# Second attention of a two-block kernel: pairs of heads, the sink as a column of the scores, outputs scaled in place of probabilities, and the exchange between two scans behind the third pair

## The chip, the cores and the metric

One core of one Trainium2 chip runs the whole program. Its engines are TensorE (PE, with its weight loads shown apart as PEld), VectorE (DVE), ScalarE (ACT), GpSimd (POOL) and SyncE (SP). The metric is the device time of one execution in microseconds (us).

## The reference

Two transformer-like blocks run one behind the other on x of 256 positions by 2048 channels, all in float32. The change touches the second block alone, which projects the normed x to queries (16 heads of 64), two key/value heads, a 512-wide input u of a state-space model and two sets of 2048 gates. Its attention looks back 127 positions, adds a linear bias by distance, and has one learned sink per head, which takes part in the softmax but has no value:

```python
scores = einsum(q, kx) * (HEAD_DIM ** -0.5) + alibi           # masked outside the window
m = jnp.maximum(jnp.max(scores, axis=-1, keepdims=True), sink)
p = jnp.exp(scores - m)
p = p / (jnp.sum(p, axis=-1, keepdims=True) + jnp.exp(sink - m))
out = einsum(p, vx)
```

The state-space model is a linear recurrence over the 256 positions with 32 groups of 64 complex states, then an output projection, GELU, a gated linear unit and a branch projection. Attention output and model output are projected, gated, summed, projected again and added to x. A feed-forward network and a norm follow.

## The kernel before

**Panels and pieces.** All large products are cut into panels of 512 output columns, and a panel into pieces of two 128-row slices of the weights. Each float32 weight is split in two parts that a fast product can take: ScalarE copies the rounded part (`weights_hi`, L1100), VectorE subtracts it from the weight to get the rest (`weights_lo`, L1617, both inputs in SBUF), and TensorE makes three products of each slice for each half of the positions (L558 to L560). A whole piece is 12 matmuls, 128x512 each. The splits run three pieces ahead of TensorE (`AHEAD`), in rings of four.

**Side work.** Small work (norms, transposes, attention, scans' inputs) is written as generators, one for each engine, and each engine advances its generator by one step behind each piece (`side.step()`). The order on every engine is thus fixed in the program, and a step that waits holds all that stands behind it on its engine: on TensorE the next piece, on ScalarE and VectorE the next split. `side.finish()` runs what is left.

**The part around the change.** Behind the panels for u, q, k and v come eight panels of gates (`gate_attn`, `gate_ssm`), 64 pieces. Side work `attention2` begins at the first of them. I number these steps from 1. Steps 1 to 4 transpose q, step 6 transposes k, and from step 7 `attention` treats the heads one by one: a step with the scores (L744, L745), a step with the output product of the head before (L765, L766), and a step that transposes the probabilities (L580). Within the step of the scores VectorE adds the bias (L1880), takes the row maxima (L1884), scales them and compares them with the sink (L1889, L1891). ScalarE takes the sink's exponential (L1317) and the exponentials with their row sums (L1320). VectorE adds the sink's part to the sum (L1898), inverts it (L1899) and multiplies the probabilities (L1901), before TensorE may transpose them. After the output product ScalarE and VectorE copy the result as two parts (L1334, L1909).

**The scans.** GpSimd makes the recurrence, in two halves, since the states fill their tile (`ssm_states`): `scan(0)`, then `scan(1)`. Each has 15 steps over all blocks, 15 small steps along the blocks, and 16 long products over 900 elements (L446, L448), all with both inputs in SBUF. Between them stands the exchange, `ssm_halves`, six steps: two output products of the first half (L944, L945, which wait for `scanned`), then four input products of the second (L927, L928), whose copies by ScalarE (L1457) release `scan(1)`. `attention` runs it behind head 8 (`if interlude and h == MIDWAY`), in steps 35 to 40. Attention's last step is 61. After the gates come two panels of four pieces (`branch_attn[0]`, `[1]`), and behind the first piece of `branch_attn[2]` `ssm_end` waits for the second scan:

```python
    def ssm_output(self, half):
        pe, ev, m = self.pe, self.ev, self.m
        pe.wait_ge(ev["scanned"], half + 1)
```

## Time and profile before

| | |
|---|---|
| median of 3 runs | 2967.99 us (2964.32 to 2967.99) |
| the profiled execution's own time | 2966.49 us |
| its span | 2965.2 us |
| PE busy | 2906.5 us (98%) |
| DVE busy | 1673.1 us (56%) |
| ACT busy | 1323.0 us (45%) |
| POOL busy | 285.3 us (10%) |
| mean granted clock of TensorE | 0.993 of full speed |
| DMA | 536.74 MB, 181 GB/s on the mean |

The span is that of one profiled execution, from its first to its last instruction. Busy time is the union of an engine's instructions, so 98% for TensorE leaves 59 us of idle time, wherever it lies. In the chain of the work that ended last TensorE holds 89%, POOL 4%, DVE 3% and ACT 2%.

### The profile page before, as it was taken

To read this page: it belongs to the slowest core of one execution; us is meant where nothing else is said; L and a number is where in the kernel's file an instruction comes from. 1 tells how busy PE (TensorE), PEld (TensorE's weight loads), DVE (VectorE), ACT (ScalarE), POOL (GpSimd) and SP (SyncE) were. 2 spreads that over 40 slices of the span, in tenths; PEclk is the share of its full clock that TensorE was granted. 3 is DMA by queue.
4 is the path that set the end of the run, shared out by engine and by line. 5 is a ranking of instruction groups with operands and counts; after the bars stand their busy time and mean duration, and the time that the engine had idled before them with its cause. 6 is when DMAs were issued, how large, how long until landed. Compare 5 with 4: busy or idle time off the path is not lost.

```text
span 2965.2 us, 32189 instructions
## 1 busy us (share of the span) xinstructions
PE 2906.5 (98%) x13246; PEld 2377.5 (80%) x13246; DVE 1673.1 (56%) x1935; ACT 1323.0 (45%) x1639; POOL 285.3 (10%) x369
## 2 busy tenths in 40 slices
PE   9999999999999999999999999996999999999998
PEld 7888887888888888888888887674788888888886
DVE  4464655555555455455555567673755666656444
ACT  5444445444444444444444454343554444444443
POOL 0000000000000000000000069296100000000000
PEclk9999999999999999999999999998999999999999
DMA  7545453555555555555666554442655555555563
GB/s 244 188 168 198 157 187 130 178 191 199 185 190 180 197 185 189 194 185 188 189 198 196 197 170 148 154 162 86 205 181 189 178 191 185 184 189 187 191 199 128
DMA packets 278464, 536.74 MB, mean 181 GB/s; under 512 B 17250, under 2 KB 19742, under 8 KB 278318
## 3 DMA queue, kind: packets, MB, share of 16 engines
q1 hardware_dynamic: 266688, 528.52, 53.3%
q10 hardware_dynamic: 11629, 6.17, 0.8%
q8 instruction: 105, 1.72, 0.2%
q14 instruction: 42, 0.34, 0.0%
HBM read 532.55 MB, written 2.10 MB: 180 GB/s over the span
## 4 chain that ended last, share of the span: by engine, by line
PE 89%; POOL 4%; DVE 3%; ACT 2%; issue 1%; DMA 0%; ACTq 0%; SPq 0%; DVEq 0%
PE panels L558 29%; PE panels L560 28%; PE panels L559 28%; PE side L580 2%; DVE weights_lo L1617 2%; POOL scan_step L423 1%; POOL ssm_states L431 1%; POOL scan_step L426 1%; POOL ssm_states L430 1%; POOL ssm_states L448 1%; ACT weights_hi L1100 1%; POOL ssm_scratch L446 1%; DMA weights<-in_w_in 0%; ACT squares L1189 0%; PE side L765 0%
## 5 line engine op out<-in xcount | busy, mean ns | idle before, releaser
L1617 DVE TENSOR_TENSOR weights_lo<-weights,weights_hi 128x1024 fp32r<-128x1024 f32 (+1 forms) x1032 | 1262.2, 1229 | 1038.4 <-ACT weights_hi L1100 1035.0
L1100 ACT ACTIVATE weights_hi<-weights 128x1024 fp32r<-128x1024 f32 (+1 forms) x1032 | 1063.5, 1035 | 1124.7 <-PE panels L560 1101.9
L558 PE MATMUL panels<-weights_hi,xT_hi 128*128 128x512 f32 (+1 forms) x2752 | 1087.9, 395 | 8.4 <-DVE weights_lo L1617 8.3
L560 PE MATMUL panels<-weights_hi,xT_lo 128*128 128x512 f32 (+1 forms) x2752 | 1070.9, 389 | 0.0
L559 PE MATMUL panels<-weights_lo,xT_hi 128*128 128x512 f32 (+1 forms) x2752 | 1069.6, 389 | 0.0
L558 PEld LDWEIGHTS panels<-weights_hi,xT_hi 128*128 128x128 f32 x2752 | 517.6, 188 | 124.5 <-issue 12.7
L560 PEld LDWEIGHTS panels<-weights_hi,xT_lo 128*128 128x128 f32 x2752 | 517.3, 188 | 108.9
L559 PEld LDWEIGHTS panels<-weights_lo,xT_hi 128*128 128x128 f32 x2752 | 518.1, 188 | 102.0 <-issue 0.2
L558 PE MATMUL panels<-weights_hi,hiddenT_hi 128*128 128x512 f32 x704 | 275.3, 391 | 1.5 <-DVE hiddenT_lo L1826 1.5
L560 PE MATMUL panels<-weights_hi,hiddenT_lo 128*128 128x512 f32 x704 | 274.1, 389 | 0.0
L559 PE MATMUL panels<-weights_lo,hiddenT_hi 128*128 128x512 f32 x704 | 274.0, 389 | 0.0
L558 PEld LDWEIGHTS panels<-weights_hi,hiddenT_hi 128*128 128x128 f32 x704 | 132.2, 188 | 28.9 <-DVE hiddenT_lo L1826 2.0
L560 PEld LDWEIGHTS panels<-weights_hi,hiddenT_lo 128*128 128x128 f32 x704 | 132.2, 188 | 27.6
L559 PEld LDWEIGHTS panels<-weights_lo,hiddenT_hi 128*128 128x128 f32 x704 | 132.2, 188 | 27.3
L382 POOL TENSOR_TENSOR rstd<-mean_squares,minus_half 128x2 f32<-128x2 f32 x5 | 3.5, 695 | 1297.0 <-DVE mean_squares L1680 1297.0
L382 POOL TENSOR_TENSOR rstd_first<-mean_squares,minus_half 128x2 f32<-128x2 f32 x1 | 0.7, 689 | 736.2 <-DVE mean_squares L1680 736.2
L423 POOL TENSOR_TENSOR scan_step<-ssm_states,ssm_vectors 128x256 f32<-128x256 f32 (+1 forms) x60 | 49.1, 818 | 84.4 <-ACT ssm_states L1457 79.9
L426 POOL TENSOR_TENSOR scan_step<-ssm_states,ssm_vectors 128x128 f32<-128x128 f32 (+1 forms) x120 | 54.0, 473 | 0.0
L431 POOL TENSOR_TENSOR ssm_states<-ssm_states,scan_step 128x256 f32<-128x256 f32 (+1 forms) x60 | 52.1, 869 | 4.7
L558 PE MATMUL panels<-weights_hi,merged2T_hi 128*128 128x512 f32 x128 | 50.8, 397 | 0.0
L558 PE MATMUL panels<-weights_hi,mixedT_hi 128*128 128x512 f32 x128 | 50.6, 395 | 0.0
L560 PE MATMUL panels<-weights_hi,merged2T_lo 128*128 128x512 f32 x128 | 50.0, 390 | 0.0
(307 smaller groups left out, 2068.8 us busy)
## 6 DMA issues: line engine op xcount, KB each, us to landing
weights<-in_w_in SPq DMA_DIRECT2D x163, 1024.0 KB, 4.9
weights<-in_w_up SPq DMA_DIRECT2D x88, 1024.0 KB, 4.8
weights<-in_w_ffn_gate SPq DMA_DIRECT2D x44, 1024.0 KB, 5.0
weights<-in_w_ffn_up SPq DMA_DIRECT2D x44, 1024.0 KB, 5.1
weights<-in_w_out SPq DMA_DIRECT2D x32, 1024.0 KB, 5.1
weights<-in_w_ffn_down SPq DMA_DIRECT2D x32, 1024.0 KB, 5.1
weights<-in_w_down SPq DMA_DIRECT2D x32, 1024.0 KB, 5.1
weights<-in_w_ffn_down SPq DMA_DIRECT2D x16, 768.0 KB, 4.5
```

The source lines that it names most:

```text
L423: pool.tensor_tensor(same, prev, row(0, 2), ALU.mult).then_inc(ev["pool_step"])
L426: pool.tensor_tensor(cross[:, c:c + 1], prev[:, 1 - c:2 - c], row(2 + c, 1), ALU.mult).then_inc(ev["pool_step"])
L430: step(pool.tensor_tensor(cur, cur, same, ALU.add))
L431: step(pool.tensor_tensor(cur, cur, cross, ALU.add))
L446: step(pool.tensor_tensor(tmp, pr, last, ALU.mult))
L448: inst = pool.tensor_tensor(cur, cur, tmp, op)
L558: pe.matmul(acc, a, wh, start=k0 + k == 0, stop=False)
L559: pe.matmul(acc, a, wl, start=False, stop=False)
L560: inst = pe.matmul(acc, b, wh, start=False, stop=k0 + k == total - 1)
L580: return self.pe.transpose(out, in_, self.m.IDENT[0:in_.shape[0], 0:in_.shape[0]])
L1100: self.act.activation(self.m.HI[:, g % PIECES, 0:n], raw, ACT.Copy).then_inc(self.ev["hi_split"])
L1617: self.dve.tensor_tensor(m.LO[:, ring, 0:n], raw, m.HI[:, ring, 0:n].bitcast(F32), ALU.subtract).then_inc(self.ev["lo_split"])
```

## The change

The second attention gets its own function, `heads2`, on TensorE, ScalarE and VectorE. The first attention keeps its instructions, only the cases for the second are taken out of `attention`.

- Heads are treated in pairs, six steps a pair: the two heads' probabilities are transposed (into banks 2 and 3), the scores of the next pair are made in one step with the two heads' products in turns, the outputs of both heads are made in one step, a step is empty for TensorE, and the scaled output is transposed.
- The sink is a column of the scores: a product of a row of ones by the sink (two columns) writes it beside each half's scores, the distance tile holds 0 there, and maxima, exponentials and row sums run over 129 and 257 columns. The sink's own instructions go. q is scaled by 1/8 when it is copied, so the scores come scaled and one negated maximum is enough.
- The probabilities stay unscaled. Their transposes are now the stationary side (128x128) and v the moving one (64 columns), so the output comes with positions on the partitions, and one VectorE instruction scales it for both heads. Two transposes turn it back.
- `MIDWAY` is 2 and counts pairs, so the exchange stands in steps 29 to 34. Attention ends in step 64.

```diff
-MIDWAY = 8
+MIDWAY = 2
+PAIRS = 8
+SCORES = 3 * P + 2
+SCORE_COLS = (slice(0, P), slice(P + 2, SCORES))
+ROW_COLS = (slice(0, P + 1), slice(P + 1, SCORES))
...
-        self.DIST2 = small("distance_in_window", [P, 3 * P])
+        self.DIST2 = small("distance_in_window", [P, SCORES])
...
-        self.SINK = small("sinks", [P, HEADS2])
...
-        self.ESINK = small("exp_sink", [P, 2, 2])
...
-        self.PR2 = sb("probabilities2", [P, 2, 3 * P], H)
+        self.PR2 = sb("probabilities2", [P, 2, SCORES], H)
+        H += 64
...
+        self.AO2 = sb("attn2", [P, TT, P], R + 100 * K)
+        self.ONES = sb("ones", [1, P], R + 101 * K)
+        self.SINK = sb("sinks", [1, HEADS2], R + 101 * K + 512)
...
-        step(pool.tensor_copy(m.DIST2[:, 0:P], m.DIST[:, 0:P]))
-        select(m.DIST2[:, P:3 * P], m.DIST[:, P:3 * P], [[1, S]], WINDOW2 - 1 - P, -1, ALU.is_ge,
+        step(pool.memset(m.DIST2[:, :], 0.0))
+        step(pool.tensor_copy(m.DIST2[:, SCORE_COLS[0]], m.DIST[:, 0:P]))
+        select(m.DIST2[:, SCORE_COLS[1]], m.DIST[:, P:3 * P], [[1, S]], WINDOW2 - 1 - P, -1, ALU.is_ge,
...
+        yield from self.heads2(scores, values)
+
+    def heads2(self, scores, values):
+        pe, m = self.pe, self.m
+        ev = self.ev.attention[1]
+
+        def pair_scores(p):
+            heads = [(h, self.bank(h % 2), *scores(h)) for h in (2 * p, 2 * p + 1)]
+            for h, ps, q, k in heads:
+                pe.matmul(ps[:, P:P + 2], m.ONES[:, :], m.SINK[:, h:h + 1].to_broadcast([1, 2]), start=True, stop=True)
+            for h, ps, q, k in heads:
+                pe.matmul(ps[:, SCORE_COLS[0]], q[:, 0:P], k[:, 0:P], start=True, stop=True)
+            for h, ps, q, k in heads:
+                pe.matmul(ps[:, SCORE_COLS[1]], q[:, P:S], k[:, 0:S], start=True, stop=True).then_inc(ev["scored"])
+                self.side_free[h % 2] = (ev["biased"], h + 1)
+
+        def turn_probabilities(h):
+            b = h % 2
+            pr = m.PR2[:, b, :]
+            ps = self.bank(2 + b)
+            pe.wait_ge(ev["exped"], h + 1)
+            self.tr(ps[:, 0:P], pr[:, SCORE_COLS[0]])
+            self.tr(ps[:, P:2 * P], pr[:, P + 2:2 * P + 2])
+            self.tr(ps[:, 2 * P:3 * P], pr[:, 2 * P + 2:SCORES]).then_inc(ev["prob_turned"])
+            self.side_free[2 + b] = (ev["probT"], h + 1)
+
+        def pair_out(p):
+            ps = self.bank(2)
+            pe.wait_ge(ev["probT"], 2 * p + 2)
+            if p:
+                pe.wait_ge(ev["out_turned"], p)
+            for b in range(2):
+                pt = m.PT2[:, b, :]
+                v0, v1 = values(2 * p + b)
+                o0, o1 = (ps[:, (2 * b + t) * DH2:(2 * b + t + 1) * DH2] for t in range(TT))
+                pe.matmul(o0, pt[:, 0:P], v0, start=True, stop=True)
+                pe.matmul(o1, pt[:, P:2 * P], v0, start=True, stop=False)
+                inst = pe.matmul(o1, pt[:, 2 * P:3 * P], v1, start=False, stop=True)
+            inst.then_inc(ev["multiplied"])
+            self.side_free[2] = (ev["out_scaled"], p + 1)
+
+        def pair_turned(p):
+            ps = self.bank(3)
+            pe.wait_ge(ev["out_scaled"], p + 1)
+            self.tr(ps[:, 0:P], m.AO2[:, 0, :])
+            self.tr(ps[:, P:S], m.AO2[:, 1, :]).then_inc(ev["out_turned"])
+            self.side_free[3] = (ev["outT_lo"], p + 1)
+
+        pe.wait_ge(self.ev["sink_row"], 1)
+        for p in range(-1, PAIRS):
+            if p >= 0:
+                turn_probabilities(2 * p)
+                yield
+                turn_probabilities(2 * p + 1)
+                yield
+            if p + 1 < PAIRS:
+                pair_scores(p + 1)
+            yield
+            if p >= 0:
+                pair_out(p)
+            yield
+            yield
+            if p >= 0:
+                pair_turned(p)
+            yield
+            if p == MIDWAY:
+                yield from self.ssm_halves()
...
-        act.wait_ge(ev.attention[1]["multiplied"], HEADS2)
+        act.wait_ge(ev.attention[1]["multiplied"], PAIRS)
...
-        act.dma_start(m.SINK[:, :], t["attn_sinks_2"][0].partition_broadcast(P)).then_inc(ev["loaded_sinks"], 16)
+        act.dma_start(m.SINK[:, :], t["attn_sinks_2"][0].partition_broadcast(1)).then_inc(ev["loaded_sinks"], 16)
...
-        act.wait_ge(ev["loaded_sinks"], 16)
-        yield from self.attention(1, HEADS2, m.OH2, DH2 ** -0.5, m.PR2, m.PT2, DH2, sink=m.SINK,
-                                  interlude=self.ssm_halves())
+        yield from self.heads2()
+
+    def heads2(self):
+        act, m = self.act, self.m
+        ev = self.ev.attention[1]
+
+        def exponentials(h):
+            b = h % 2
+            act.wait_ge(ev["neg_max"], h + 1)
+            for t in range(TT):
+                pr = m.PR2[:, b, ROW_COLS[t]]
+                inst = act.activation(pr, pr, ACT.Exp, bias=m.NM[:, b, t:t + 1], accum_out=m.RSUM[:, b, t:t + 1])
+            inst.then_inc(ev["exped"])
+
+        def copy_probabilities(h):
+            b = h % 2
+            act.wait_ge(ev["prob_turned"], h + 1)
+            if h >= 2:
+                act.wait_ge(ev["multiplied"], h // 2)
+            act.activation(m.PT2[:, b, :], m.SIDE[:, 2 + b, 0:3 * P], ACT.Copy).then_inc(ev["probT"])
+
+        def pair_hi(p):
+            act.wait_ge(ev["out_turned"], p + 1)
+            act.activation(m.OH2[:, p, :], m.SIDE[:, 3, 0:S], ACT.Copy).then_inc(ev["outT_hi"])
+
+        for p in range(-1, PAIRS):
+            if p >= 0:
+                copy_probabilities(2 * p)
+                yield
+                copy_probabilities(2 * p + 1)
+                yield
+            yield
+            if p + 1 < PAIRS:
+                exponentials(2 * p + 2)
+            yield
+            if p + 1 < PAIRS:
+                exponentials(2 * p + 3)
+            yield
+            if p >= 0:
+                pair_hi(p)
+            yield
+            if p == MIDWAY:
+                yield from self.ssm_halves()
...
-                                         m.V3[:, k:k + 1], None, ALU.add)
+                                         m.V3[:, k:k + 1], DH2 ** -0.5, ALU.add, ALU.mult)
...
+        dve.memset(m.ONES[:, :], 1.0).then_inc(ev["sink_row"])
...
-        yield from self.attention(1, HEADS2, (m.OH2, m.OL2), m.DIST2, lambda h: 2.0 ** (-8.0 * (h + 1) / HEADS2),
-                                  DH2 ** -0.5, m.PR2, DH2, sink=m.SINK, interlude=self.ssm_halves())
+        yield from self.heads2()
+
+    def heads2(self):
+        dve, m = self.dve, self.m
+        ev = self.ev.attention[1]
+
+        def row_max(h):
+            b = h % 2
+            pr = m.PR2[:, b, :]
+            dve.wait_ge(ev["scored"], h + 1)
+            if h >= 2:
+                dve.wait_ge(ev["prob_turned"], h - 1)
+            dve.scalar_tensor_tensor(out=pr, in0=m.DIST2[:, :], scalar=-2.0 ** (-8.0 * (h + 1) / HEADS2),
+                                     in1=m.SIDE[:, b, 0:SCORES], op0=ALU.mult, op1=ALU.add).then_inc(ev["biased"])
+            dve.wait_ge(ev["biased"], h + 1)
+            for t in range(TT):
+                inst = dve.tensor_reduce(m.NM[:, b, t:t + 1], pr[:, ROW_COLS[t]], AX, ALU.max, negate=True)
+            inst.then_inc(ev["neg_max"])
+
+        def inverse(p):
+            dve.wait_ge(ev["exped"], 2 * p + 2)
+            self.step(dve.reciprocal(m.RINV[:, :, :], m.RSUM[:, :, :]))
+
+        def scale_out(p):
+            dve.wait_ge(ev["multiplied"], p + 1)
+            if p:
+                dve.wait_ge(ev["out_turned"], p)
+            dve.tensor_tensor(m.AO2[:, :, :].rearrange("p t (b d) -> p b t d", d=DH2),
+                              m.SIDE[:, 2, 0:2 * TT * DH2].rearrange("p (b t d) -> p b t d", t=TT, d=DH2),
+                              m.RINV[:, :, :].unsqueeze(3).to_broadcast([P, 2, TT, DH2]),
+                              ALU.mult).then_inc(ev["out_scaled"])
+
+        def pair_lo(p):
+            dve.wait_ge(ev["outT_hi"], p + 1)
+            dve.tensor_tensor(m.OL2[:, p, :], m.SIDE[:, 3, 0:S], m.OH2[:, p, :].bitcast(F32),
+                              ALU.subtract).then_inc(ev["outT_lo"])
+
+        for p in range(-1, PAIRS):
+            if p >= 0:
+                inverse(p)
+                yield
+                yield
+            if p + 1 < PAIRS:
+                row_max(2 * p + 2)
+            yield
+            if p + 1 < PAIRS:
+                row_max(2 * p + 3)
+            yield
+            if p >= 0:
+                scale_out(p)
+            yield
+            if p >= 0:
+                pair_lo(p)
+            yield
+            if p == MIDWAY:
+                yield from self.ssm_halves()
```

`tr` is a transpose on TensorE, `bank(b)` waits until bank `b` of the side's PSUM is free, and `step` on VectorE waits for its own instruction.

## Rows read from the trace of the kernel before

**Rows 1.** The page's 40 slices: busy tenths of TensorE and GpSimd, granted clock of TensorE
```profile
PE   9999999999999999999999999996999999999998
POOL 0000000000000000000000069296100000000000
PEclk9999999999999999999999999998999999999999
```

**Rows 2.** Waits, 1700 to 2070 us: who waited for whom, total us, times, longest
```profile
ACT exp_sink L1317 <- DVE minus_max L1891: 81.6, 15, 11.7
...
PE side L944 <- POOL ssm_states L448: 26.0, 1, 26.0
```

**Rows 3.** Chain of waits, 2048 to 2070 us: start, us, what
```profile
2053.68 1.93 POOL ssm_states L448
```

**Rows 4.** Timeline of GpSimd: start us, us, operation [idle before <-releaser]; first scan, second's start
```profile
1728.75 0.77 POOL L423 TENSOR_TENSOR scan_step<-ssm_states,ssm_vectors 128x256 f32<-128x256 f32 x1 [26.54 <-ACT ssm_states L1457]
...
1867.21 2.81 POOL L448 TENSOR_TENSOR ssm_states<-ssm_states,ssm_scratch 128x900 f32<-128x900 f32 x1
...
1923.35 0.77 POOL L423 TENSOR_TENSOR scan_step<-ssm_states,ssm_vectors 128x256 f32<-128x256 f32 x1 [53.32 <-ACT ssm_states L1457]
```

**Rows 5.** Timeline of TensorE: step 29, and the exchange's first, second and last step
```profile
1879.61 0.48 PE L744 MATMUL side<-kT,qT 64*128 64x128 f32 x2
...
1900.94 0.66 PE L944 MATMUL side<-ssm_states,cT_re 128*32 128x256 f32 x8
...
1904.95 0.66 PE L944 MATMUL side<-ssm_states,cT_re 128*32 128x256 f32 x8
...
1921.55 0.60 PE L928 MATMUL side<-uT,bbT_im 32*128 32x256 f32 x4
```

**Rows 6.** VectorE's L1617 in each scan: count, ns least/median/most, first and last start
```profile
L1617 DVE TENSOR_TENSOR weights_lo<-weights,weights_hi x44: 1208/1508/2981, 1729.7 to 1869.5; 128x1024 fp32r<-128x1024 f32 x44
...
L1617 DVE TENSOR_TENSOR weights_lo<-weights,weights_hi x33: 1206/1298/2485, 1924.2 to 2029.0; 128x1024 fp32r<-128x1024 f32 x33
```

**Rows 7.** Timeline of GpSimd: one form alone, and beside a split of VectorE
```profile
1796.68 0.87 POOL L430 TENSOR_TENSOR ssm_states<-ssm_states,scan_step 128x256 f32<-128x256 f32 x1
...
1800.22 1.88 POOL L430 TENSOR_TENSOR ssm_states<-ssm_states,scan_step 128x256 f32<-128x256 f32 x1
```

**Rows 8.** Timeline of TensorE: first scores, and panel starts behind side work
```profile
1792.16 0.49 PE L744 MATMUL side<-kT,qT 64*128 64x128 f32 x2
...
1810.48 0.50 PE L558 MATMUL panels<-weights_hi,xT_hi 128*128 128x512 f32 x1
...
1813.62 0.48 PE L558 MATMUL panels<-weights_hi,xT_hi 128*128 128x512 f32 x1
...
1817.40 0.50 PE L558 MATMUL panels<-weights_hi,xT_hi 128*128 128x512 f32 x1
...
1821.14 0.50 PE L558 MATMUL panels<-weights_hi,xT_hi 128*128 128x512 f32 x1
```

**Rows 9.** Windows: length; PE, PEld, DVE, ACT, POOL busy; TensorE's clock; DMA share, GB/s
```profile
1996.70:2029.60 32.90, 32.90 (x145) 26.95 (x144) 20.74 (x19) 17.13 (x17) 30.43 (x74) 1.00 0.47 160
...
2029.70:2055.60 25.90, 0.00 (x0) 0.00 (x0) 0.96 (x1) 0.63 (x1) 24.95 (x13) 0.57 0.06 20
...
2055.70:2059.00 3.30, 3.30 (x20) 1.78 (x21) 1.08 (x2) 0.00 (x0) 0.00 (x0) 0.50 0.00 0
```

**Rows 10.** Timeline of TensorE: the last exchange step behind the long wait
```profile
2055.65 1.10 PE L944 MATMUL side<-ssm_states,cT_re 128*32 128x256 f32 x8 [25.98 <-POOL ssm_states L448]
...
2061.94 0.44 PE L944 MATMUL side<-ssm_states,cT_re 128*32 128x256 f32 x4
```

**Rows 11.** Waits, 1792 to 1880 us, of TensorE for a split
```profile
PE panels L558 <- DVE weights_lo L1617: 6.5, 4, 2.8
```

**Rows 12.** Timeline of VectorE while GpSimd runs its long products
```profile
1838.24 1.75 DVE L1898 TENSOR_TENSOR row_sum<-row_sum,exp_sink 128x2 f32<-128x2 f32 x1
```

More of the change, by code:

```diff
@@ L109, in __init__ @@
         self.loaded = [sem(f"loaded_weights{i}") for i in range(SLOTS)]
-        self.attention = [{n: sem(f"{n}_{i}") for n in self.ATTENTION} for i in (1, 2)]
+        self.attention = [{n: sem(f"{n}_{i + 1}") for n in self.ATTENTION[i]} for i in range(2)]
     def __getitem__(self, name):
@@ L734, in a_down, with attention @@
         yield
-    def attention(self, which, heads, scores, values, ptile, ptT, dh, interlude=None):
+    def attention(self, heads, scores, values, ptile, ptT):
         pe, m = self.pe, self.m
-        ev = self.ev.attention[which]
+        ev = self.ev.attention[0]
         def head_scores(h):
@@ L758, in head_out @@
             pt = ptT[:, h % 2, :]
-            rows = slice(0, P) if dh == P else slice(dh * (h % 2), dh * (h % 2) + dh)
-            if dh == P or h % 2 == 0:
-                self.bank(3)
-            o = m.SIDE[rows, 3, 0:S]
+            o = self.bank(3)[:, 0:S]
             pe.wait_ge(ev["probT"], h + 1)
@@ L782, in attention @@
                 yield
-            if interlude and h == MIDWAY:
-                yield from interlude
     def attention1(self):
@@ L801, in attention1 @@
         yield from self.attention(
-            0, HEADS, lambda h: (m.QT[:, h, :], m.KT[:, h, :]),
-            lambda h: [m.TB[:, t, 2 * BW + h * DH:2 * BW + (h + 1) * DH] for t in range(TT)], m.PR, m.PT, DH)
+            HEADS, lambda h: (m.QT[:, h, :], m.KT[:, h, :]),
+            lambda h: [m.TB[:, t, 2 * BW + h * DH:2 * BW + (h + 1) * DH] for t in range(TT)], m.PR, m.PT)
     def gla(self):
@@ L985, in values @@
             return [m.VV[:, i, c:c + DH2] for i in range(TT)]
-        yield from self.attention(1, HEADS2, scores, values, m.PR2, m.PT2, DH2, interlude=self.ssm_halves())
+        yield from self.heads2(scores, values)
[59 more added lines that the diff above has]
+                yield from self.ssm_halves()
@@ L1307, in a_down, with attention @@
         act.activation(m.ADT[:, :], m.SIDE[0:RANK, 0, 0:S], ACT.Copy).then_inc(ev["adt_ready"])
-    def attention(self, which, heads, out, scale, ptile, ptT, dh, sink=None, interlude=None):
+    def attention(self, heads, out, scale, ptile, ptT):
         act, m = self.act, self.m
-        ev = self.ev.attention[which]
+        ev = self.ev.attention[0]
         def head_scores(h):
@@ L1330, in head_out @@
         def head_out(h):
-            if dh != P and h % 2 == 0:
-                return
             act.wait_ge(ev["multiplied"], h + 1)
-            act.activation(out[:, h if dh == P else h // 2, :], m.SIDE[:, 3, 0:S], ACT.Copy).then_inc(ev["outT_hi"])
+            act.activation(out[:, h, :], m.SIDE[:, 3, 0:S], ACT.Copy).then_inc(ev["outT_hi"])
         head_scores(0)
@@ L1347, in attention @@
                 yield
-            if interlude and h == MIDWAY:
-                yield from interlude
     def attention1(self):
@@ L1358, in attention1 @@
                 yield
-        yield from self.attention(0, HEADS, m.OH, DH ** -0.5, m.PR, m.PT, DH)
+        yield from self.attention(HEADS, m.OH, DH ** -0.5, m.PR, m.PT)
     def gla(self):
@@ L1867, in a_down, with attention @@
             yield
-    def attention(self, which, heads, out, dist, slope, scale, ptile, dh, sink=None, interlude=None):
+    def attention(self, heads, out, dist, slope, scale, ptile):
         dve, m = self.dve, self.m
-        ev = self.ev.attention[which]
+        ev = self.ev.attention[0]
         regions = ((slice(0, P), 0), (slice(P, 3 * P), 1))
@@ L1885, in head_scores @@
             self.settle()
-            if sink is None:
-                dve.tensor_scalar(m.NM[:, b, :], m.RMAX[:, b, :], -scale, None, ALU.mult).then_inc(ev["neg_max"])
-            else:
-                self.step(dve.tensor_scalar(m.RMAX[:, b, :], m.RMAX[:, b, :], scale, sink[:, h:h + 1],
-                                            ALU.mult, ALU.max))
-                dve.tensor_scalar(m.NM[:, b, :], m.RMAX[:, b, :], -1.0, None, ALU.mult).then_inc(ev["neg_max"])
+            dve.tensor_scalar(m.NM[:, b, :], m.RMAX[:, b, :], -scale, None, ALU.mult).then_inc(ev["neg_max"])
         def head_norm(h):
@@ L1896, in head_norm @@
             dve.wait_ge(ev["exped"], h + 1)
-            if sink is not None:
-                self.step(dve.tensor_tensor(m.RSUM[:, b, :], m.RSUM[:, b, :], m.ESINK[:, b, :], ALU.add))
             self.step(dve.reciprocal(m.RINV[:, b, :], m.RSUM[:, b, :]))
@@ L1904, in head_out @@
         def head_out(h):
-            if dh != P and h % 2 == 0:
-                return
-            tile = h if dh == P else h // 2
-            dve.wait_ge(ev["outT_hi"], tile + 1)
-            dve.tensor_tensor(out[1][:, tile, :], m.SIDE[:, 3, 0:S], out[0][:, tile, :].bitcast(F32),
+            dve.wait_ge(ev["outT_hi"], h + 1)
+            dve.tensor_tensor(out[1][:, h, :], m.SIDE[:, 3, 0:S], out[0][:, h, :].bitcast(F32),
                               ALU.subtract).then_inc(ev["outT_lo"])
@@ L1925, in attention @@
                 yield
-            if interlude and h == MIDWAY:
-                yield from interlude
     def attention1(self):
@@ L1936, in attention1 @@
                 yield
-        yield from self.attention(0, HEADS, (m.OH, m.OL), m.DIST, lambda h: 2.0 ** (-8.0 * (h + 1) / HEADS),
-                                  DH ** -0.5, m.PR, DH)
+        yield from self.attention(HEADS, (m.OH, m.OL), m.DIST, lambda h: 2.0 ** (-8.0 * (h + 1) / HEADS),
+                                  DH ** -0.5, m.PR)
     def gla(self):
```

11 lines of the change are left out of this document (5 added, 6 removed).

## Prediction

> **What bounds the kernel now.** I read the page's 40 slices first. TensorE is at nine tenths or more everywhere but in slice 28, where it falls to six tenths and its granted clock falls too, and GpSimd is busy in slices 24 to 29 alone [rows 1]. So almost everywhere the TensorE products are the bound, and one hole stands beside GpSimd's scans. The waits of that stretch name it: TensorE waited once, 26.0 us, for `ssm_states`, the end of the second scan; and ScalarE waited 81.6 us in 15 heads for VectorE's maximum [rows 2]. The chain then shows which of the two sets the time: its last link before TensorE resumes is GpSimd's last product, 2053.68 to 2055.61 [rows 3]. What delays that product delays the end, and what TensorE does between the start of the second scan and the hole is free as long as the hole stays.
>
> So I follow GpSimd. Its first scan starts at 1728.75 and ends at 1867.21 + 2.81 = 1870.02; it then stands idle 53.3 us until 1923.35 [rows 4]. TensorE reaches the exchange only at 1900.94 [rows 5]. The path is: first scan 141.3 us, nothing for 30.9 us (until TensorE comes to step 35), exchange 22.4 us (1900.94 to 1923.35), second scan 132.3 us (to 2055.61). Together 326.9 us.
>
> **The change part by part.** Three edits bear on this path: where the exchange stands, how early TensorE gets there, and how many splits fall into each scan. The rest lies beside it.
>
> *The exchange, moved from step 35 to step 29.* In the run before, step 29 was reached at 1879.61 [rows 5], which is 9.6 us behind the first scan's end. In the new kernel TensorE gets there sooner, for two reasons. First, the side work is smaller. From the starts of panel work: with one head's scores a piece takes 1817.40 - 1813.62 = 3.78 us, with one head's output 3.74, with three transposes 3.14 [rows 8], and 12 pieces without side work take 32.9 us, 2.74 each [rows 9]. So scores cost 1.04 us a head, output 1.00, three transposes 0.40: 4.9 us a pair of heads. In the new kernel:
> - Scores of a pair: at best the two heads' products, which use different halves of the rows, run side by side and the sink costs nothing, 1.04; at worst all is serial, 2.08, and four passes for the sinks come on top at 0.11 each (0.40 us for three transposes, so 0.11 to 0.13 a pass), 2.5. I take 1.5: the products of two row groups are in turns, so most of it should overlap, and the sinks use the same rows.
> - Output of a pair: 6 products, 12 passes, each with 128 columns of weights to load. By the transposes' 0.11 a pass this is 1.3; by the row before, 2.0 for two heads. I take 1.4, nearer to the transposes, whose weights have the same shape.
> - Transposes: two of 0.40 as before, and 0.25 for the two of the output.
>
> That is 3.95 us a pair, 0.9 less. Step 7 began at 1792.16 [rows 8]. Steps 7 to 28 are 22 pieces, 60.3 us, and hold 4 score steps (6.0), 6 transposed heads (2.4), 3 outputs (4.2) and 3 turned outputs (0.75): TensorE is at step 29 at 1865.8, between 1863 and 1871 by the bounds. Second, this holds no stall. Before, TensorE stood 6.5 us for splits in this stretch [rows 11], in the time of GpSimd's long products, when a two-column sum of VectorE took 1.75 us [rows 12]. These sums and the scaling of the probabilities, both held up by GpSimd, are gone, and VectorE no longer makes ScalarE wait inside a step, as maximum and exponential stand a step apart. If the stalls came back, TensorE would be there at 1872 to 1875 and the sum below would hardly change.
>
> So TensorE comes before the first scan has ended. The 30.9 us of nothing go, and a new wait stands in their place: TensorE for the first scan. Behind it in TensorE's queue is the piece of step 30; VectorE waits in the same step for the output product, with the split for step 33 behind it; nobody else needs either.
>
> *Splits in the scans.* GpSimd's same form took 0.87 us alone and 1.88 when it met a split [rows 7]. First scan 141.3 us with 44 splits, second 132.3 with 33 [rows 6]; the rest of the two scans is the same work. The difference, 9.0 us for 11 splits, gives 0.8 us a split, the pair of rows 1.0; I take 0.9. How many splits fall into a scan follows from the program: TensorE is held at step 29 and the splits run three ahead, so the first scan now sees those up to step 32. Before, TensorE was in step 26 when the scan ended and the splits stood at step 28. That is 4 more: +3.6 us, the first scan ends at 1873.7 (1870 to 1876). The second scan always ends with TensorE waiting and all splits made up to three pieces past `branch_attn[2]`'s first. It started behind step 40's piece, now behind step 34's: 6 more splits, 39, so 132.3 + 5.4 = 137.7 us.
>
> The Trainium skill has a rule on this, "SBUF — State Buffer", section "Who interferes with whom": a VectorE instruction with two SBUF inputs and a GpSimd instruction that reads SBUF exclude each other for a whole instruction, and the loser is fully blocked. By that rule each split would cost its own length instead of the 0.9 of the rows; the rows speak for a price a little below that, since some splits fall into GpSimd's gaps. It also speaks against moving the exchange forward, as each step forward brings one more split into the scan.
>
> *The exchange itself.* 22.4 us as before, if TensorE runs at full clock. But it will have waited for some 8 us. Behind the wait of 26 us the granted clock is 0.50, so 1.2 GHz [rows 9], and the output step took 2061.94 - 2055.65 = 6.3 us [rows 10] where it took 4.0 at the full clock (1904.95 - 1900.94, [rows 5]): +2.3 us. The floor is 0, if TensorE comes late enough. I take 24.7: the second scan starts at 1873.7 + 24.7 = 1898.4 and ends at 2036.1. That is 19.5 us before 2055.6.
>
> *Does TensorE still wait there?* From step 29 there are 44 pieces, 120.6 us, the exchange's products (two output steps of 1.27 and, by the same spacing, four input steps of about 1.3: 7.7), the clock's 2.3, and for attention four score steps 6.0, ten transposed heads 4.0, five outputs 7.0, five turned outputs 1.25. Attention's end is late now: its last step is that of the last gate piece, and TensorE waits there for a copy on ScalarE and one on VectorE, some 1.2 us that were hidden before by three pieces. Sum 150.1, so TensorE is at the wait at 2023.8 (2031 by the upper bounds), and waits 12 us, which covers all of these terms. So nothing of the side work saved behind the exchange shows in the time.
>
> *Costed at nothing:* the maximum and exponentials over 129 and 257 columns, the second operation on q's copy, the row of ones, the smaller load of the sinks (issued in step 1, wanted in step 5), one more fill by GpSimd at the start (its first want is 30 us on). GpSimd is idle, or TensorE's hole covers them; without cover each is under 0.6 us.
>
> *The sum.* 141.3 + 3.6 + 24.7 + 137.7 = 307.3 us in place of 326.9. What follows the second scan runs as before, and in it TensorE is dense. The profiled execution took 2966.5 us, so 2947.0 is its counterpart; the median of the runs shown is 1.5 us above it: **2948.5 us**.
>
> **The rivals.**
> - *Dearer splits or starved pieces.* If each split costs its shortest own length, 1.2 us [rows 6], the ten more cost 12 instead of 9, and the old splits don't change; with VectorE held up so long by GpSimd's products that TensorE loses the 6.5 us of [rows 11] and 3 us of clock again, now at the end of the second scan, and with the upper bounds of side work, TensorE arrives at 2040. Either way 2952. For it: that stretch was just so before. Against it: VectorE's blocked instructions are now one a step.
> - *Cheap waits.* The new wait doesn't cost the clock and the splits cost 0.5: 2948.5 - 2.3 - 4 = 2942. For it: some of the splits before were held up themselves and cost GpSimd nothing. Against it: rows 7 and 10.
> - *Slower than before: a wait in each pair.* A turned output needs VectorE's scaling of one step before, which stands in VectorE's queue behind a split that GpSimd's products hold. If that comes a whole piece late, TensorE stands for it in each of the five pairs behind the exchange, and loses clock each time. The hole has room for 12 us, and the gain is 19.5: from 6.3 us a pair on the kernel is slower. At 8 us (two pieces' time 5.5, clock 2.3) it would take 2976. Against it: the scaling has more than a piece's time, 2.74 us, and needs under 0.5.
> - *The change doesn't reach the end:* TensorE gives back behind the scan what it gained, 2966. Nothing in [rows 1] shows a second bound there.
>
> **How the numbers follow.** Forecast 64%, dearer or starved 15%, cheap waits 12%, a wait in each pair 4%, no effect 5%. Two medians of this kernel can be told apart from 0.2%, 6 us. Faster by more: the first three and a part of the last, 0.92; within: 0.04; slower: 0.04. The forecast's own range is 2944 to 2952; with the two cases beside it and the runs' spread of 3.7 us, 2939 to 2957.
>
> **What would show it.** The second scan starts near 1898 and ends near 2036; the first ends near 1874 with 48 splits in it, the second has 39. TensorE waits for `ssm_states` twice, some 8 us in step 29 and some 12 us in `branch_attn[2]`. ScalarE's waits for VectorE's maximum all but go. A pair's score step costs 1.5 us and its output step 1.4. The forecast is wrong if the second scan starts later than 1905, if TensorE doesn't wait for it, or if either scan is longer than 145 us.

## The result, and the profile after

| | before | new |
|---|---|---|
| median | 2967.88 us (2964.32 to 2967.99, 4 runs) | 2946.27 us (2945.51 to 2947.7, 4 runs) |
| ratio to before | | 0.993 (0.9914 to 0.9946) |
| span of the profiled execution | 2965.2 us | 2946.4 us |

The new kernel is 21.6 us faster by the medians, and 18.8 us by the spans of the two profiled executions. The forecast was 2948.5 us.

In the 40 slices of the page the hole beside GpSimd's scans, six tenths before [rows 1], is now two nicks of eight tenths, one for each wait, and no slice shows TensorE's clock below nine tenths:

```profile
PE   9999999999999999999999999898999999999998
...
POOL 0000000000000000000000059696100000000000
...
PEclk9999999999999999999999999999999999999999
```

The waits of the new kernel, 1700 to 2070 us (who waited for whom, total us, times, longest):

```profile
PE side L947 <- POOL ssm_states L457: 20.6, 2, 11.8
...
ACT probabilities L1562 <- DVE minus_max L2276: 11.4, 9, 1.5
```

TensorE waits for GpSimd twice now, 20.6 us in all, where it had waited once for 26.0; and ScalarE's waits for the maximum fell from 81.6 us to 11.4 [rows 2]. The timeline of GpSimd has the two scans' first and last operations, and behind the idle time in brackets what ended it:

```profile
1730.25 0.77 POOL L432 TENSOR_TENSOR scan_step<-ssm_states,ssm_vectors 128x256 f32<-128x256 f32 x1 [26.54 <-ACT ssm_states L1520]
...
1874.02 1.92 POOL L457 TENSOR_TENSOR ssm_states<-ssm_states,ssm_scratch 128x900 f32<-128x900 f32 x1
...
1900.45 0.77 POOL L432 TENSOR_TENSOR scan_step<-ssm_states,ssm_vectors 128x256 f32<-128x256 f32 x1 [24.51 <-ACT ssm_states L1520]
...
2035.49 1.92 POOL L457 TENSOR_TENSOR ssm_states<-ssm_states,ssm_scratch 128x900 f32<-128x900 f32 x1
```

The first scan runs from 1730.25 to 1875.94, the second from 1900.45 to 2037.41 [rows 4 has the starts of before]. The splits in each scan (VectorE's L1720 now; count, then shortest, median and longest in ns, first and last start) are 48 and 39, where they were 44 and 33 [rows 6]:

```profile
L1720 DVE TENSOR_TENSOR weights_lo<-weights,weights_hi x48: 1211/1514/2867, 1731.2 to 1865.8; 128x1024 fp32r<-128x1024 f32 x48
...
L1720 DVE TENSOR_TENSOR weights_lo<-weights,weights_hi x39: 1212/1468/2985, 1901.4 to 2026.3; 128x1024 fp32r<-128x1024 f32 x39
```

On TensorE's timeline the first four rows give the price of the pair's work, as the starts of panel work did before [rows 8]; the other four are the first two output steps, the end of attention and the last wait:

```profile
1809.34 0.48 PE L567 MATMUL panels<-weights_hi,xT_hi 128*128 128x512 f32 x1
...
1812.27 0.60 PE L999 MATMUL side<-sinks,ones 1*128 1x2 f32 x4
...
1813.66 0.50 PE L567 MATMUL panels<-weights_hi,xT_hi 128*128 128x512 f32 x1
...
1817.81 0.48 PE L567 MATMUL panels<-weights_hi,xT_hi 128*128 128x512 f32 x1
...
1875.99 1.11 PE L947 MATMUL side<-ssm_states,cT_re 128*32 128x256 f32 x8 [8.83 <-POOL ssm_states L457]
...
1882.06 0.66 PE L947 MATMUL side<-ssm_states,cT_re 128*32 128x256 f32 x8
...
2000.91 0.50 PE L567 MATMUL panels<-weights_hi,attn2T_hi 128*128 128x512 f32 x1 [1.44 <-DVE attn2T_lo L2294]
...
2037.47 1.11 PE L947 MATMUL side<-ssm_states,cT_re 128*32 128x256 f32 x8 [11.78 <-POOL ssm_states L457]
```

A pair's score step takes 1813.66 - 1809.34 = 4.32 us with its piece, so 1.58 us for itself, of which the sinks have 0.53 (1812.27 to 1812.80). Its output step takes 4.15 us, 1.41 for itself. The windows of the wait and of the 3 us behind it (length; PE, PEld, DVE, ACT, POOL busy; granted clock; DMA share, GB/s) show what the wait costs beyond itself, a granted clock of 0.50, which is 1.2 GHz:

```profile
1867.20:1875.90 8.70, 0.00 (x0) 0.00 (x0) 1.23 (x1) 1.06 (x1) 8.39 (x5) 0.68 0.36 121
...
1876.00:1879.00 3.00, 3.00 (x19) 1.59 (x20) 0.95 (x2) 0.00 (x0) 0.00 (x0) 0.50 0.02 5
```

The path, by term:

| | before | forecast | new |
|---|---|---|---|
| first scan | 141.3 | 144.9 | 145.7 |
| waiting for TensorE | 30.9 | 0 | 0 |
| exchange | 22.4 | 24.7 | 24.5 |
| second scan | 132.3 | 137.7 | 137.0 |
| sum, us | 326.9 | 307.3 | 307.2 |

### The profile page after: what moved, and what is told of

The parts are those of the page before. It is cut to its first block, busy times and chain, and to the rows that moved or that the text cites. A ratio compares the mean times of both kernels' runs of the same rounds, so it can differ in the third digit from the quotient of the medians.

```text
span 2946.4 us, 32285 instructions
## 1 busy us (share of the span) xinstructions
PE 2898.7 (98%) x13326; PEld 2383.6 (81%) x13326; DVE 1650.3 (56%) x1856; ACT 1324.2 (45%) x1623; POOL 295.0 (10%) x370
## 4 chain that ended last, share of the span: by engine, by line
PE 87%; POOL 9%; ACT 1%; DVE 1%; issue 1%; DMA 0%; ACTq 0%; SPq 0%; DVEq 0%; POOLq 0%
PE panels L567 28%; PE panels L569 28%; PE panels L568 28%; PE side L589 2%; POOL scan_step L432 2%; POOL scan_step L435 2%; POOL ssm_states L440 2%; POOL ssm_states L439 1%; POOL ssm_states L457 1%; POOL ssm_scratch L455 1%; DMA weights<-in_w_in 0%; DVE weights_lo L1720 0%; ACT weights_hi L1169 0%; ACT squares L1258 0%; PE side L871 0%
## 5 line engine op out<-in xcount | busy, mean ns | idle before, releaser
L1720 DVE TENSOR_TENSOR weights_lo<-weights,weights_hi 128x1024 fp32r<-128x1024 f32 (+1 forms) x1032 | 1271.1, 1237 | 1042.4 <-ACT weights_hi L1169 1038.9
```

The costliest lines, as they stand in the source:

```text
L1720: self.dve.tensor_tensor(m.LO[:, ring, 0:n], raw, m.HI[:, ring, 0:n].bitcast(F32), ALU.subtract).then_inc(self.ev["lo_split"])
```

## The experiments

My theory is that the end of this stretch is set by GpSimd's path: first scan, exchange, second scan, where a split of VectorE in a scan makes it longer by 0.9 us. The main rival is that the lighter side work on TensorE made the gain. Others are named with their runs. The kernels of a group ran on one chip and share the runs of the kernel before, whose medians were 2967.6 us (first group: runs 1 to 4), 2965.75 (second: a_one, a_warm, a_dense, a_all) and 2966.5 (third: a_warm38, a_all2). The new kernel was not run again in these groups, so a difference of some 2 us between a run and the new kernel's 2946.27 says nothing by itself: the medians of the kernel before differ by as much.

**1. The exchange's place alone** (b_mid6, the kernel before):

```diff
-MIDWAY = 8
+MIDWAY = 6
```

> The kernel before with one number changed: the exchange stands behind head 6 in place of head 8, so in steps 29 to 34 as in the new kernel; heads stay single. Theory (the path is first scan, exchange, second scan, and 0.9 us for each split in a scan): TensorE comes to step 29 at 1879.6 us as before, behind the first scan's end, so it does not wait there and keeps its clock; exchange 22.4 us, second scan from 1902 with 39 splits, 137.7 us, to 2040: 16 us less than before, 2952 us. Rival (the lighter attention is what gained): nearly all of the gain is missing, 2964 us or more.

Measured 2950.41 us (2949.26 to 2950.83), ratio 0.9944 (0.9932 to 0.9957). The second scan's start on GpSimd's timeline, its splits, and TensorE's waits:

```profile
1902.56 0.77 POOL L423 TENSOR_TENSOR scan_step<-ssm_states,ssm_vectors 128x256 f32<-128x256 f32 x1 [32.95 <-ACT ssm_states L1457]
```

```profile
L1617 DVE TENSOR_TENSOR weights_lo<-weights,weights_hi x39: 1207/1496/2986, 1903.5 to 2030.8; 128x1024 fp32r<-128x1024 f32 x39
```

```profile
PE side L944 <- POOL ssm_states L448: 9.9, 1, 9.9
...
PE panels L558 <- DVE weights_lo L1617: 6.4, 4, 2.8
```

The second scan starts at 1902.6, with 39 splits, and ends at 2040.06, 137.5 us later. The waits of TensorE for splits are as before, 6.4 us [rows 11], and nothing is lighter, and still four fifths of the gain are there. The rival falls for this half.

**2. The pairs alone** (a_mid3, the new kernel with the exchange where it was, in steps 35 to 40):

```diff
-MIDWAY = 2
+MIDWAY = 3
```

> The new kernel with the exchange behind the fourth pair, steps 35 to 40, where it was before. Theory: TensorE comes to step 35 at 1867.2 + 6 x 2.74 + 3.9 = 1887.5 us, without a wait; exchange 22.4, second scan from 1910 with 33 splits, 132.3 us, to 2042.2: 4.8 us later than in the new kernel, 2951 us. The pairs alone so make 17 us of the 21. Rival (the place of the exchange is what gained): near 2964 us.

Measured 2950.90 us (2950.08 to 2953.01), ratio 0.9948 (0.9934 to 0.9961).

```profile
1907.87 0.77 POOL L432 TENSOR_TENSOR scan_step<-ssm_states,ssm_vectors 128x256 f32<-128x256 f32 x1 [32.02 <-ACT ssm_states L1520]
```

```profile
L1720 DVE TENSOR_TENSOR weights_lo<-weights,weights_hi x33: 1214/1308/1871, 1908.8 to 2010.8; 128x1024 fp32r<-128x1024 f32 x33
```

```profile
PE side L947 <- POOL ssm_states L457: 27.2, 1, 27.2
```

The rival "the place alone" falls too: the pairs bring TensorE to step 35 at 1885.5 in place of 1900.9, and that makes 16.7 us. The second scan, with 33 splits as before, took 131.6 us. TensorE's last wait is 27.2 us, about as long as before the change (26.0): it saved side work before and behind the exchange, but only what was saved before it reached the time. The two halves, 17.2 and 16.7 us, don't add up to 34, because the first scan's end stops what both do together: they bring TensorE to the exchange sooner, and from 1876 on that is worth nothing.

**3. Earlier still** (a_mid1, exchange in steps 23 to 28, `MIDWAY = 1`):

> The new kernel with the exchange behind the second pair, steps 23 to 28. Theory: TensorE comes at 1847 and waits 24 us; held there, it lets only 42 splits into the first scan (48 in the new kernel), which ends at 1871 in place of 1876; the second scan has 45 in place of 39 and takes 142 us, to 2037.5, as in the new kernel. But TensorE, held six steps earlier, comes to its last wait only at 2041: 3.5 us later, 2950 us, and no wait for the second scan. Rival (the number of splits doesn't set a scan's length, 145.7 and 137.0 stay): the first scan ends at 1876, TensorE is late by 9 us, 2955 us.

Measured 2947.62 us (2946.05 to 2947.9), ratio 0.9934 (0.9921 to 0.9946). The splits of both scans, the last row of the first scan, the start and last row of the second, and TensorE's first product behind it:

```profile
L1720 DVE TENSOR_TENSOR weights_lo<-weights,weights_hi x42: 1211/1484/2314, 1730.7 to 1845.0; 128x1024 fp32r<-128x1024 f32 x42
...
L1720 DVE TENSOR_TENSOR weights_lo<-weights,weights_hi x43: 1214/1355/2978, 1894.9 to 2032.4; 128x1024 fp32r<-128x1024 f32 x43
```

```profile
1868.16 1.92 POOL L457 TENSOR_TENSOR ssm_states<-ssm_states,ssm_scratch 128x900 f32<-128x900 f32 x1
...
1893.99 0.77 POOL L432 TENSOR_TENSOR scan_step<-ssm_states,ssm_vectors 128x256 f32<-128x256 f32 x1 [23.91 <-ACT ssm_states L1520]
...
2031.44 2.82 POOL L457 TENSOR_TENSOR ssm_states<-ssm_states,ssm_scratch 128x900 f32<-128x900 f32 x1
```

```profile
2039.04 0.66 PE L947 MATMUL side<-ssm_states,cT_re 128*32 128x256 f32 x8
```

As expected the first scan has 42 splits and ends at 1870.08, 140.3 us long; TensorE, held 23.8 us there, comes to its last wait at 2039.0, 4.8 us after the second scan has ended at 2034.26, and waits no more. The second scan had 43 splits and not 45, since it ended before TensorE had come so far, and took 140.3 us in place of 142. The time is 1.4 us above the new kernel's, within the spread of the runs. So the chosen place lies on a flat bottom: one pair earlier TensorE's panel work is the bound, one later GpSimd's path is 4 us longer.

**4. Side work on TensorE doubled in one part** (a_serial): the products of one head, then those of the other.

```diff
             for h, ps, q, k in heads:
                 pe.matmul(ps[:, P:P + 2], m.ONES[:, :], ...)
-            for h, ps, q, k in heads:
                 pe.matmul(ps[:, SCORE_COLS[0]], q[:, 0:P], k[:, 0:P], start=True, stop=True)
-            for h, ps, q, k in heads:
                 pe.matmul(ps[:, SCORE_COLS[1]], ...)
```

> The new kernel with the products of a pair's scores in the order of the heads: all of one head, then all of the other, so that row groups no longer alternate. Theory: a score step costs some 0.6 us more (up to 2.2 in place of 1.4), which lies under TensorE's waits of 8.8 and 11.8 us: no change, 2946 us, and the waits shorter by 2.4 and 2.4 us. Rival (TensorE's side work is on the path): 8 x 0.6 = 5 us slower, 2951 us.

Measured 2945.68 us (2945.03 to 2947.31), ratio 0.9930 (0.9918 to 0.9943): no change. The waits of TensorE for the two scans:

```profile
PE side L947 <- POOL ssm_states L457: 12.9, 2, 7.9
```

They fell from 20.6 to 12.9 us. By the starts of panel work a score step with its piece now takes 5.24 us (1808.72 to 1813.96) in place of 4.32, so 0.92 more (I had said 0.6), 7.4 us for the eight. So over 7 us of additional work on TensorE cost nothing in this stretch, as the waits covered them.

**5. Splits that do not meet GpSimd** (a_one). For the 92 pieces around the scans VectorE's instruction has one SBUF input; what is left out is said in the expectation.

```diff
+        if 608 <= g < 700:
+            self.dve.tensor_reduce(m.LO[:, ring, 0:n], m.HI[:, ring, 0:n].bitcast(F32).unsqueeze(2), AX,
+                                   ALU.add).then_inc(self.ev["lo_split"])
+            return
         self.dve.tensor_tensor(m.LO[:, ring, 0:n], raw, m.HI[:, ring, 0:n].bitcast(F32), ...
```

> The new kernel in which VectorE's splits of the pieces around the two scans (92 of 1032, at the same places) are a reduction over an axis of one element, with one input in SBUF; the subtraction is left out there, so the low part of those weights is wrong. Theory (a split stretches GpSimd's operation only since both have their inputs in SBUF and exclude each other): both scans shrink by what their splits cost, 48 and 39 times 0.9 us, to some 102 us each; the first ends at 1832, TensorE comes to the exchange at 1867 without a wait, the second ends at 1990, and TensorE comes to its last wait at 2014.6: no wait for GpSimd is left, 23 us less than the new kernel, 2923.5 us. Rival (GpSimd is stretched by something else than the splits): scans stay at 146 and 137 us and the time at 2946 us.

Measured 2920.43 us (2920.24 to 2920.46), ratio 0.9847 (0.9834 to 0.9860). First and last operation of each scan on GpSimd's timeline, and the instruction in place of the split in the first scan:

```profile
1728.17 0.77 POOL L432 TENSOR_TENSOR scan_step<-ssm_states,ssm_vectors 128x256 f32<-128x256 f32 x1 [26.54 <-ACT ssm_states L1520]
...
1828.53 1.95 POOL L457 TENSOR_TENSOR ssm_states<-ssm_states,ssm_scratch 128x900 f32<-128x900 f32 x1
...
1886.90 0.77 POOL L432 TENSOR_TENSOR scan_step<-ssm_states,ssm_vectors 128x256 f32<-128x256 f32 x1 [56.42 <-ACT ssm_states L1520]
...
1986.17 1.95 POOL L457 TENSOR_TENSOR ssm_states<-ssm_states,ssm_scratch 128x900 f32<-128x900 f32 x1
```

```profile
L1722 DVE TENSOR_REDUCE weights_lo<-weights_hi x38: 1206/1219/1221, 1729.1 to 1828.8; 128x1024 fp32r<-128x1024 f32 x38
```

The scans take 102.3 and 101.2 us. The replaced instruction is as long as an undisturbed split (1.22 us), stands at the same places and was never held up itself (1.206 to 1.221 us where splits took up to 2.87), so the number and length of VectorE's instructions is not what stretches GpSimd. The run changes two things at once, the inputs and the operation (a reduction for a subtraction). The new kernel's trace parts them on VectorE's side: its subtraction L2294, with one input in SBUF and one in PSUM, took 0.41 to 0.43 us all eight times, and so was never held up, while the splits took up to 2.99. That a subtraction with one SBUF input would leave GpSimd alone too was not run. The price of a split is (145.7 - 102.3)/48 = 0.90 us in the first scan and (137.0 - 101.2)/39 = 0.92 in the second. These are averages. One form of GpSimd's in the new kernel, beside a split that ran from 1799.87 to 1801.09, and alone:

```profile
1799.94 1.91 POOL L440 TENSOR_TENSOR ssm_states<-ssm_states,scan_step 128x256 f32<-128x256 f32 x1
...
1810.91 0.88 POOL L440 TENSOR_TENSOR ssm_states<-ssm_states,scan_step 128x256 f32<-128x256 f32 x1
```

In the first scan's block steps (1730 to 1812 us) its 128x256 operations are either at their own length, to within 0.05 us, or longer by 0.84 to 1.08 us. Without the two-input splits no wait of TensorE for GpSimd is left, and the kernel's time is some 25 us below the new kernel's.

**6. The clock behind the new wait** (a_warm and a_warm38): products of the identity before the exchange keep TensorE busy while it would wait.

```diff
     def ssm_halves(self):
+        self.bank(3)
+        self.warm(28)          # 38 in a_warm38
         yield from self.ssm_output(0)
```

> The new kernel with 28 products of the identity by itself on TensorE (6.1 us) between its arrival at step 29 and its wait for the first scan. Theory: TensorE's idle time before the exchange falls from 8.8 to 2.7 us or less, its granted clock stays at 2.4 GHz or nearly so, and the exchange takes 22.4 us in place of 24.5: 2 us less, 2944 us. Rival (the longer exchange has another cause than the clock): 24.5 us as before, 2946 us.

> As a_warm, with 38 products (8.3 us) in place of 28, since 2.6 us of idle time left the exchange at 24.0 us and the granted clock at 0.56 behind it. Theory: with 0.5 us of idle time the granted clock stays at 1.0, the exchange takes 22.4 us, 2 us less than in the new kernel, 2944 us. Rival (the first output step behind a scan is longer for another reason): 24 us again, 2946 us.

Measured 2945.41 us (2943.59 to 2947.52), ratio 0.9932 (0.9919 to 0.9944), with 28, and 2944.59 us (2943.71 to 2945.09), ratio 0.9925 (0.9911 to 0.9939), with 38. The first 3 us of the exchange, with 28 and with 38, and the second scan's start with 38:

```profile
1874.40:1877.40 3.00, 3.00 (x19) 1.74 (x20) 1.30 (x2) 0.00 (x0) 0.00 (x0) 0.56 0.00 0
```

```profile
1874.30:1877.30 3.00, 3.00 (x25) 2.11 (x26) 1.62 (x2) 0.00 (x0) 0.00 (x0) 1.00 0.00 0
```

```profile
1896.64 0.77 POOL L432 TENSOR_TENSOR scan_step<-ssm_states,ssm_vectors 128x256 f32<-128x256 f32 x1 [22.44 <-ACT ssm_states L1522]
```

With 28 products 2.6 us of idle time were left, the granted clock behind it was 0.56, and the exchange took 24.0 us: the expectation was missed. With 38 the idle time was 0.35 us, the clock stayed at 1.00, and the exchange took 22.44 us, as before the change (22.4). So the 2.1 us are the clock's. (In run 4, with 5.0 us of idle time, the exchange took 24.0 us.) The times differ by less than the runs spread, so the gain is shown in the trace and not in the medians.

**7. A shorter exchange** (a_dense): all of it in step 29. On TensorE, and alike on ScalarE and VectorE:

```diff
     def ssm_halves(self):
-        yield from self.ssm_output(0)
-        yield from self.ssm_input(1)
+        for _ in self.ssm_output(0):
+            pass
+        for _ in self.ssm_input(1):
+            pass
+        yield
```

> The new kernel with the whole exchange in step 29: both output steps and all input products one behind the other, without the five pieces of panel work between them. Theory: the exchange takes some 9.5 us in place of 24.5 (TensorE at 1.2 GHz for its first 3 us, then the pace of ScalarE's eight copies); five more splits fall into the second scan, 137.0 + 4.4 = 141.4; it ends at 1876 + 9.5 + 141.4 = 2027, while TensorE comes at 2024: 10.5 us less, 2936 us. Rival (with its pieces held up, TensorE becomes the bound, or ScalarE's copies hold up its splits): the wait at the second scan is gone and the time stays above 2940 us.

Measured 2934.43 us (2932.91 to 2936.92), ratio 0.9895 (0.9882 to 0.9909). GpSimd's second scan, first and last operation:

```profile
1885.26 0.77 POOL L432 TENSOR_TENSOR scan_step<-ssm_states,ssm_vectors 128x256 f32<-128x256 f32 x1 [9.68 <-ACT ssm_states L1523]
...
2023.91 2.78 POOL L457 TENSOR_TENSOR ssm_states<-ssm_states,ssm_scratch 128x900 f32<-128x900 f32 x1
```

The exchange took 9.7 us and the second scan, with 44 splits, 141.4 us; TensorE still waited 4.0 us at its end. The terms came as reckoned (9.5 and 141.4 us), the time 1.6 us below the 2936 expected.

**8. All hand-overs to GpSimd in one step** (a_all, a_all2). In a_all, besides a_dense's exchange, the inputs of the first scan and both last output steps are made dense in the same way. In a_all2 empty steps put the transposes of the output weights back to where they were.

> As a_dense, and the inputs of the first scan in one step too (its transposes of u in one step, its products in the next), and both output steps of the second half in one step, with three pieces between them and the use of the GELU's result. Theory: the first scan starts 8 us earlier; TensorE waits less at step 29 by as much; splits in the scans 51 and 44. Path: 1722 + 148 + 9.5 + 141.4 = 2021, and the last 1.4 us of TensorE's waiting for the GELU go: 16.5 + 1.4 = 18 us less than the new kernel, 2928.5 us. Rival (TensorE then is the bound): it comes to the second scan's end at 2018 or later without a wait, and the time is above 2930 us.

> As a_all, with the transposes of the output weights back at their old steps, since TensorE had waited 5.0 us there for their transfer. Theory: TensorE comes to step 29 at 1868, as the first scan ends (1720.6 + 147.2), so without a wait of over 1 us and at 2.4 GHz; the exchange takes 8.5 us in place of 12.7, the second scan ends at 1876.3 + 141.4 = 2017.7: 4 us less than a_all, 2926 us. Rival (TensorE is the bound by now): it comes to the second scan's end later than the scan, and the time stays at 2930 us.

a_all measured 2930.29 us (2929.62 to 2932.45), ratio 0.9883 (0.9868 to 0.9898). Its waits of TensorE name what I had missed:

```profile
PE side L589 <- DMA c_twice<-in_ssm_c_im: 5.0, 1, 5.0
...
PE side L949 <- POOL ssm_states L457: 4.0, 1, 4.0
```

Moved four steps forward, the transposes waited 5.0 us for their transfer, TensorE came to the exchange 5.4 us behind the first scan's end, and 12.7 us passed between the scans in place of the 9.5 expected: 5.4 until TensorE came and 7.3 for the exchange itself. The time is 1.8 us above the 2928.5 expected. With the steps put back (a_all2) it is 2925.93 us (2924.73 to 2926.33), ratio 0.9862 (0.9849 to 0.9876), 40.6 us below the kernel before and about 20 below the change. GpSimd's scans in a_all2, and TensorE's waits for them:

```profile
1720.41 0.76 POOL L432 TENSOR_TENSOR scan_step<-ssm_states,ssm_vectors 128x256 f32<-128x256 f32 x1 [18.64 <-ACT ssm_states L1531]
...
1866.17 1.93 POOL L457 TENSOR_TENSOR ssm_states<-ssm_states,ssm_scratch 128x900 f32<-128x900 f32 x1
...
1875.52 0.77 POOL L432 TENSOR_TENSOR scan_step<-ssm_states,ssm_vectors 128x256 f32<-128x256 f32 x1 [7.42 <-ACT ssm_states L1531]
...
2014.14 2.78 POOL L457 TENSOR_TENSOR ssm_states<-ssm_states,ssm_scratch 128x900 f32<-128x900 f32 x1
```

```profile
PE side L950 <- POOL ssm_states L457: 4.5, 2, 4.0
```

TensorE came to the exchange 0.5 us before the first scan ended, kept its clock (1.00 from 1869 to 1876), and the exchange took 7.4 us (8.5 expected). The second scan ended at 2016.9, and 4.0 us of waiting are left.

## Why the prediction was right

- **What bounds the stretch.** Shown by runs 1 to 4: moving the exchange moves the end as GpSimd's path says (2950.4 and 2950.9 us against 2952 and 2951 expected), and 7.7 us more of TensorE's work move nothing.
- **TensorE comes before the first scan has ended.** It was there at 1867.2, 1.4 us later than reckoned, in a trace in which step 7 began 1.4 us later (1793.57) than before. Steps 7 to 28 took 73.6 us, as forecast, where they had taken 87.5. The stalls for splits are gone: 6.5 us before [rows 11], none in the new kernel between 1792 and 1866. Of the 13.9 us so gained the stalls are nearly half, and behind one of them, 2.5 us long, the granted clock before had been 0.58 for 3 us. The lighter products alone would have brought less. Which of the edits removed the stalls (the sink's own instructions, the scaling of the probabilities, or the step between maximum and exponential) no run separates.
- **The price of a split**, 0.9 us, is what run 5 measured, 0.90 and 0.92. The counts, 48 and 39, came out as counted in the program. What the forecast took from one pair of rows and one difference was the right size. The Trainium skill's rule of exclusion ("SBUF — State Buffer", section "Who interferes with whom"), priced as the prediction did with a split's whole length, would have made it 1.2. Run 5 agrees with the rule's condition, two SBUF inputs on VectorE's side, and the operations that are either not stretched or stretched by 0.84 to 1.08 us look like exclusion and not like sharing; only the price of a whole length was a third too high.
- **The exchange**, 24.7 forecast and 24.5 measured, is 22.4 plus 2.1 us of clock, shown by run 6.
- **TensorE's work.** Score step 1.5 forecast, 1.58 measured; output step 1.4, 1.41. Without the sinks' 0.53 us the score step is 1.05, its lower bound of 1.04; the output step's lower bound was 1.3. The overlap of the two heads is worth 0.92 us a pair (run 4), so without it the score step is 2.5 us, the upper bound.
- **The last wait** was 11.8 us, 12 forecast. The end of attention showed as a wait of 1.4 us (1.2 forecast), covered as said.
- **The rivals.** No pair of the new attention waits ("slower than before"). Of "dearer splits" and "cheap waits" nothing came: the splits cost neither 1.2 nor 0.5 us, no stall came back, and the clock did fall behind the new wait. "The change doesn't reach the end" falls by the medians.
- **What the medians add.** The traces give 19.7 us on the path, of which the first scan's start takes back 1.5; that is spread between executions, since in other runs of the new kernel with nothing changed ahead of it the scan starts between 1728.2 and 1729.9. The profiled execution of the kernel before was 1.4 us faster than its median (2966.49 against 2967.88), that of the new kernel 1.4 us slower (2947.7 against 2946.27), so the medians give 21.6 where the two traces give 18.8. For the profiled execution the forecast was 2947.0, 0.7 us too low; its 2948.5 lies 2.2 us above the median, since it set the median 1.5 us above the profiled execution and it came 1.4 us below.

## What to carry to other kernels

Where one engine's hole stands beside another engine's long chain, take the chain as the path and count its terms: its own work, the hand-overs, and what other engines' instructions do to it while it runs; savings on the waiting engine count only up to a hand-over, and only until the chain's previous link has ended. Work spread thin so as to be hidden (a step for each piece) is dear at a hand-over to the chain: five pieces between two scans cost 15 us here, and making the hand-overs dense gave nearly as much as the whole change, some 20 us. Before an early start is bought on an engine that shares something with the chain, count what it now runs beside: here 0.9 us for each of ten more splits.

## What the runs showed of the hardware

- A VectorE subtraction with both inputs in SBUF (1.22 us alone) stretched GpSimd's operations, which read SBUF too, by 0.90 to 0.92 us each on the mean, a single one of 128x256 by 0.84 to 1.08; a VectorE reduction of the same size with one input in SBUF stretched them by nothing (scans of 102.3 and 101.2 us, 1.22 us for each reduction throughout).
- 2.6 us without work left TensorE's granted clock at 0.56 in the 3 us behind it, 8.8 us left it at 0.50, and 0.35 us at 1.00.
- Products of two heads on different halves of the rows, issued in turns, overlapped nearly in full: 1.05 us for the two without the sinks' 0.53, against 1.04 for one head before. Issued head by head they cost 0.92 us more.
- A product with one row of weights and two columns to stream took 0.13 us a pass (0.53 us for the four of a pair), though it streams next to nothing.
